# Fewer sums in the last pass of the first branch, its first tokens brought forward, and another order in the final block: one core of a hybrid GLA and Fourier layer

## What is computed

```python
h = _rmsnorm(x, norm_g) * (1 + scale) + shift
z = h @ w_in                      # q, k, v, gates, u, merge gates
...                               # gated linear attention: o; Fourier mixing: four
y_a = (o * silu(gate_a)) @ w_proj_a
y_b = (four * silu(gate_b)) @ w_proj_b
merged = sigmoid(mg_a) * y_a + sigmoid(mg_b) * y_b
x = x + gate * (merged @ w_out)
y = _rmsnorm(x, final_norm_g)
```

## Time and profile before

| what | value |
| --- | --- |
| median of three runs | 1940.96 us (1940.04 to 1943.69) |
| the profiled execution, its own time | 1941.48 us |
| its span, first to last instruction | 1939.7 us |
| busy: PE, DVE, ACT, POOL | 97%, 62%, 49%, 32% |
| mean granted clock of PE | 0.989 of full |

### The profile page before, as it was taken

The page is one execution under the profiler, slowest core; times in us unless marked ns, Lnnn a source line. Parts: engine busy times, 40 slices in busy tenths (PEclk is TensorE's granted clock), DMA queues, the critical chain, the costliest instruction groups (busy, mean ns, idle before and its releaser), DMA issues.

```text
span 1939.7 us, 30160 instructions
## 1 busy us (share of the span) xinstructions
PE 1876.0 (97%) x10393; PEld 1755.2 (90%) x10393; DVE 1211.3 (62%) x2103; ACT 941.2 (49%) x1961; POOL 620.3 (32%) x668
## 2 busy tenths in 40 slices
PE   7899999999999999999999998999999989998997
PEld 2899999999999999999999996888887889997886
DVE  4978887784444435644444455666665567599787
ACT  3565667653445446444455325777741242243343
POOL 0136644044334513345432000000931014233644
PEclk9999999999999999999999999999999999999998
DMA  7578878967788889778778969565447657765443
GB/s 286 209 271 291 284 284 317 369 245 255 249 280 284 254 302 349 240 227 290 261 263 291 351 194 362 211 236 218 167 184 238 217 169 228 254 206 176 163 163 130
DMA packets 170096, 483.24 MB, mean 249 GB/s; under 512 B 14880, under 2 KB 72666, under 8 KB 159964
## 3 DMA queue, kind: packets, MB, share of 16 engines
q1 hardware_dynamic: 156124, 430.99, 64.7%
q10 hardware_dynamic: 13824, 50.34, 6.5%
HBM read 316.64 MB, written 155.20 MB: 243 GB/s over the span
## 4 chain that ended last, share of the span: by engine, by line
PE 60%; DVE 8%; POOL 4%; DMA 3%; issue 3%; ACT 2%; SPq 0%; DVEq 0%; ACTq 0%; POOLq 0%
PE bank L2543 33%; PE bank L2889 7%; PE bank L2843 5%; PE bank L2707 3%; PE bank L2674 3%; PE bank L2772 2%; PE bank L2685 1%; PE bank L2696 1%; DMA x_st<-in_x 1%; POOL h_lo L1127 1%; DVE me_op L2164 1%; POOL yt L1261 1%; POOL yt L1258 1%; DVE me_s L2316 1%; DMA qd<-qk_dec 1%
## 5 line engine op out<-in xcount | busy, mean ns | idle before, releaser
L2543 PE MATMUL bank<-h_hi,w_op 128*128 128x384 f32 x4032 | 1053.3, 337 | 15.2 <-ACT outs L1340 4.6
L2543 PEld LDWEIGHTS bank<-h_hi,w_op 128*128 128x128 f32 x4032 | 732.6, 188 | 21.4 <-issue 21.3
L2543 PE MATMUL bank<-h_lo,w_op 128*128 128x384 f32 x2016 | 675.8, 335 | 0.0
L2543 PEld LDWEIGHTS bank<-h_lo,w_op 128*128 128x128 f32 x2016 | 380.3, 189 | 0.0
L1831 DVE TENSOR_TENSOR w_op<-w_raw,w_op 128x512 fp32r<-128x512 f32 x240 | 189.0, 788 | 96.8 <-ACT w_op L1300 93.4
L1152 POOL TENSOR_TENSOR decs<-decs,qk_s 128x192 f32<-128x192 f32 x192 | 123.3, 677 | 333.2 <-ACT decs L1374 332.9
L1300 ACT ACTIVATE w_op<-w_raw 128x512 fp32r<-128x512 f32 x240 | 149.3, 624 | 159.2 <-PE bank L2543 155.6
L2889 PE MATMUL bank<-op_a,a_op 128*128 128x384 f32 x1008 | 180.2, 340 | 9.1 <-issue 5.0
L2889 PEld LDWEIGHTS bank<-op_a,a_op 128*128 128x128 f32 x1008 | 179.3, 192 | 9.9 <-issue 5.4
L2922 PE MATMUL bank<-ow_op,me_op 128*128 128x512 f32 x756 | 176.8, 395 | 9.0 <-DVE u4o L2394 4.3
L2922 PEld LDWEIGHTS bank<-ow_op,me_op 128*128 128x128 f32 x756 | 142.8, 190 | 42.5 <-issue 7.7
(11 more groups left out here) (272 smaller groups left out, 2829.5 us busy)
## 6 DMA issues: line engine op xcount, KB each, us to landing
w_op<-wt_dram SPq DMA_DIRECT2D x192, 512.0 KB, 5.7
wt_dram<-w_op ACTq DMA_DIRECT2D x96, 512.0 KB, 4.6
w_raw<-in_w_in SPq DMA_DIRECT2D x48, 768.0 KB, 5.9
w_raw<-in_w_in SPq DMA_DIRECT2D x24, 1024.0 KB, 6.7
qk_dec<-decs SPq DMA_DIRECT2D x48, 384.0 KB, 6.5
mg_dram<-outs SPq DMA_DIRECT2D x24, 768.0 KB, 7.4
swap<-qk_s SPq DMA_DIRECT2D x48, 192.0 KB, 5.6
v_dram<-outs SPq DMA_DIRECT2D x24, 384.0 KB, 4.8
```

The lines of the kernel that those rows point to most:

```text
L2543: ins = pe.matmul(bnk, w_op[slot][:, part, k, :], h[:, j, k, :], start=(first and k == 0 and part == 0 and h is h_hi), stop=(k == HK - 1 a ...
```

## The change

**The output weights' sums** are no longer made from the whole weights in the last pass of the first branch. In windows 2, 6, 10 and 14 of the projection's second pass SP loads a quarter (one of the four k-tiles) of the four blocks of `w_out` (`load_ow_parts`), into places that the second pass leaves unused; in the window after, DVE makes the four sums of that quarter (`sum_ow_part`, 128x512 each), and in the one after that SP stores them to the new `ow_dram`. In the first branch's last pass SP then loads seven ready tiles (`load_ow`), three from `w_out` and four from `ow_dram`, where before it loaded four. The places of the tiles (`OW_LO`, `OW_HI`) are others, and high and low parts of the first two tiles are made a step earlier.

**The first branch's first tokens**: `top` is loaded at tile 26 of the second branch, not 29; the low parts of its last block are made at tile 24, not 27; `low_op(0)` and the first two `sum_tokens` stand behind tiles 34, 36 and 38, not behind tile 39.

**The final block**: DVE takes the quarter that frees the bank of PE's seventh product before the two sums that don't, and PE waits for one DVE instruction less.

```diff
+        ow_parts = Region(r1.at - 2048)("ow_parts", [P, 4, 512])
+        ow_first = Region(r1.at - 10240)("ow_first", [P, 512])
...
-        OW_LO = (A_LO[0], A_HI[2], A_LO[2], A_HI[0], A_HI[1], A_LO[1], A_LO[3])
-        OW_HI = (A_HI[3], A_LO[4], A_HI[4], A_LO[5], A_HI[5], A_LO[6], A_HI[6])
-        OW_STEP = (3, 4, 4, 5, 5, 6, 6)
-        ow_b11, ow_t2, ow_t1, ow_b12, ow_b21, ow_b22, ow_t4 = ow_src = [place(at, f"ow_src{j}", [P, HK, 512])
-                                                                      for j, at in enumerate(OW_LO)]
+        OW_LO = (A_LO[0], A_HI[0], A_LO[1], A_HI[1], A_LO[2], A_LO[3], A_LO[4])
+        OW_HI = (A_HI[2], A_HI[3], A_HI[4], A_LO[5], A_HI[5], A_LO[6], A_HI[6])
+        OW_READ = (0, 0, 1, 1, 2, 3, 4)
+        OW_STEP = (2, 3, 4, 5, 5, 6, 6)
+        ow_src = [place(at, f"ow_src{j}", [P, HK, 512]) for j, at in enumerate(OW_LO)]
...
+        OW_WINDOWS = (2, 6, 10, 14)
...
-        END = {"u2": AD + 1, "u4": AD + 2, "t12": AD + 4, "t21": AD + 6, "t22": AD + 8, "22": AD + 10, "11": AD + 12,
+        END = {"u2": AD + 1, "u4": AD + 2, "t22": AD + 4, "22": AD + 6, "t12": AD + 8, "t21": AD + 10, "11": AD + 12,
...
+            def load_ow_parts(part):
+                if part:
+                    sp.wait_ge(s_wr[1], 32 * part)
+                else:
+                    sp.wait_ge(s_wlo, split_count(NW - 1, NPROD - 1))
+                sp.dma_start(ow_parts[:, :, :], io["w_out"][:, :, part, :].rearrange("q p n -> p q n")).then_inc(s_wr[0], 16)
+
+            def store_ow_sums(part):
+                sp.wait_ge(s_owl, 4 * part + 4)
+                sp.dma_start(ow_dram[0, :, part, :], ow_first[:, :]).then_inc(s_wr[1], 16)
+                sp.dma_start(ow_dram[1:4, :, part, :].rearrange("q p n -> p q n"), ow_parts[:, 1:4, :]).then_inc(s_wr[1], 16)
...
+                    if p == 1 and w in OW_WINDOWS:
+                        load_ow_parts(OW_WINDOWS.index(w))
+                    elif p == 1 and w - 2 in OW_WINDOWS:
+                        store_ow_sums(OW_WINDOWS.index(w - 2))
...
-            def load_ow(k):
-                sp.dma_start((ow_b11, ow_b21, ow_b22, ow_b12)[k][:, :, :], io["w_out"][k]).then_inc(s_wr[k], 16)
+            def load_ow(j):
+
+                sp.wait_ge(s_y, product_a(NPROD * (NA - 1) + OW_READ[j], 3))
+                sp.wait_ge(s_wr[OW_SLOT[j]], ow_read(j) - 16)
+                src = (io["w_out"][0], ow_dram[2], ow_dram[0], ow_dram[3], io["w_out"][1], io["w_out"][2], ow_dram[1])[j]
+                sp.dma_start(ow_src[j][:, :, :], src).then_inc(s_wr[OW_SLOT[j]], 16)
...
-                if m == 29:
+                if m in (26, 29):
                     sp.wait_ge(s_bil, GROUPS * NB)
-                    load_tokens_a(0, 0)
-                    load_tokens_a(0, 1)
+                    load_tokens_a(0, int(m == 29))
...
-                        sp.wait_ge(s_y, product_a(NPROD * (NA - 1), 3))
                         load_ow(0)
-                        load_ow(3)
+                        load_ow(1)
+                    elif at == 4:
+                        load_ow(4)
+                        load_ow(5)
...
-                        sp.wait_ge(s_y, product_a(NPROD * (NA - 1) + 1, 3))
                         load_ow(2)
-                        load_ow(1)
+                        load_ow(3)
+                    elif at == 6:
+                        load_ow(6)
...
-                    for j in {4: (0,), 5: (1, 2), 6: (3, 4)}.get(i, ()):
+                    for j in {3: (0,), 4: (1,), 5: (2,), 6: (3, 4)}.get(i, ()):
...
+            def sum_ow_part(part, n):
+                b11, b21, b22, b12 = (ow_parts[:, q, :] for q in range(4))
+                out, x, y = ((ow_first[:, :], b12, b11), (b12, b12, b22), (b22, b22, ow_first[:, :]), (b21, b21, b22))[n]
+                if n:
+                    dve.wait_ge(s_owl, 4 * part + n)
+                else:
+                    dve.wait_ge(s_wr[0], 16 * (part + 1))
+                dve.tensor_tensor(out, x, y, ALU.subtract).then_inc(s_owl, 1)
...
+                        if p == 1 and w - 1 in OW_WINDOWS and 0 < j < 5:
+                            sum_ow_part(OW_WINDOWS.index(w - 1), j - 1)
...
-                if j == 3 and b + 1 < NB:
+                if (b, j) in ((0, 3), (1, 3), (2, 3), (3, 0)):
                     for g in range(GROUPS):
                         low_fourier(b + 1, g)
                 elif (b, j) in ((1, 1), (1, 6)):
                     for n in ((0, 1) if j == 1 else (2, 3)):
                         sum_a(n)
-                elif (b, j) in ((2, 2), (2, 6), (3, 1)):
-                    low_a(((2, 2), (2, 6), (3, 1)).index((b, j)))
-            low_op(0)
+                elif (b, j) in ((2, 2), (2, 6), (3, 3)):
+                    low_a(((2, 2), (2, 6), (3, 3)).index((b, j)))
+                elif b == NB - 1 and j == 2:
+                    low_op(0)
+                elif b == NB - 1 and j in (4, 6):
+                    sum_tokens(0, j // 2 - 2)
...
-                if i in (0, 2):
+                if step and i in (0, 2):
...
-                        sum_ow(0)
-                        sum_ow(1)
-                        sum_ow(2)
-                    elif i == 4:
-                        sum_ow(3)
+                        low_ow(0)
                         for n in range(3):
                             sum_me(0, n)
-                        low_ow(0)
-                    elif i == 5:
+                    elif i == 4:
                         low_me(0, 0)
                         low_ow(1)
+                    elif i == 5:
...
-            scaled_sum(y[0][:, sl[1]], u2o[:, :], 0, 1, END["u4"])
             dve.wait_ge(s_yst[1], 16 * (FINAL - 1))
+            scaled_sum(y[1][:, sl[1]], u4o[:, :], 1, 1, END["u4"])
+            end_quarter(1, 1, 3, 3, y[1][:, sl[1]], END["t22"])
+            scaled_sum(y[0][:, sl[1]], u2o[:, :], 0, 1, END["22"])
             scaled_sum(y[1][:, sl[0]], u2o[:, :], 1, 0, END["t12"])
-            scaled_sum(y[1][:, sl[1]], u4o[:, :], 1, 1, END["t21"])
-            end_quarter(1, 1, 3, 3, y[1][:, sl[1]], END["t22"])
             scale_rows(FINAL - 1, 1)
-            end_quarter(0, 0, 0, 4, x_end[0][:, sl[0]], END["22"])
+            end_quarter(0, 0, 0, 4, x_end[0][:, sl[0]], END["t21"])
...
-                    pe.wait_ge(s_owl, 4 + j + 1)
+                    pe.wait_ge(s_owl, 4 * 4 + j + 1)
...
-                    pe.wait_ge(s_ad, END["u4"] if j == 5 else END["22"])
+                    pe.wait_ge(s_ad, END["u4"] if j == 5 else END["22"] - 1)
```

35 lines of the change are left out of this document (11 added, 24 removed).

## The result

The changed kernel takes 1930.32 us (median of 4 runs, 1926.61 to 1931.80) beside 1941.43 for the kernel before (4 runs, 1940.04 to 1943.69): a ratio of 0.9939, with a 95% interval of 0.9922 to 0.9956. By the ratio that is 11.8 us faster, between 8.5 and 15.1 (the medians themselves differ by 11.1). In two later series of runs the same kernel stood at 0.9946 [0.9924, 0.9968] and 0.9945 [0.9932, 0.9958]. The forecast was 13.2 us and 1928; the range of 1922.5 to 1933 held the time. The profiled execution took 1931.80 us, its span 1930.0.

What follows compares the result with a forecast made beforehand. PE was busy 97% of the span, so time could be won only where it waits or runs slowly. 7.5 + 4.6 + 1.4 - 0.3 = 13.2 us off 1941.48 gave 1928.3, predicted as 1928 us; 8-in-10 range 1922.5 to 1933.

Steps and rivals of the forecast that it cites:

- Part A: Entry to the first branch: PE's 5.0 us wait and 2.5 us of slow clock behind it go; 7.5 us won.
- Part B: Last pass and first output block: `u4a` wait and its slow clock go, `u4o` wait grows; 4.6 us won.
- the long waits grow: First output block: PE's wait for `u4o` grows from 3.3 to 5.0 us.
- later small waits absorb: Output: PE's next two waits, 1.0 and 1.12 us, would absorb 2.1 us of the slow clock's cost.
- I count nothing; if they hold DVE, part B shrinks: Last pass: seven weight loads, 7 MB for 4, share the queue with DVE's gate tiles; no cost counted.
- a sign against itself: First output block: a `u4o` wait as before or gone, not about 5 us, would mean DVE's chain was misread.
- Rival 2: Heavier loads or the first output block give Part B back, PE's clock included: 1932 us; chance 15%.
- Part C: Final block: PE's 3.3 us wait goes and PE ends 6.0 us earlier, but the end comes only 1.4 earlier.
- Part D: Projection's second pass: 16 added sums, 13 us of DVE, and their transfers stay nearly hidden; 0.3 us lost.
- Rival 3: Entry to the first branch: gates, tokens and sums crowd, the second step waits: 1933 us, at worst 1935.5; chance 10%.
- rival 4: Projection: quarters of `w_out` arrive so late that DVE stands; slower, 1966 us; chance 4%.
- rival 1: DVE keeps nearly all it is given, so Part B gives 8 to 12 us: 1924 us, at best 1921; chance 10%.

Runs made afterwards that it cites:

- e8: The changed kernel with both loads of the first branch's first tokens at tile 29, as before the change; 0.9939 of the kernel before.
- a2_after: The changed kernel unaltered, run and profiled a second time; 0.9946 of the kernel before.
- a3_after: The changed kernel unaltered, run and profiled a third time; 1928.32 us, 0.9945 of the kernel before.
- e4: The changed kernel with the seventh weight tile's 1 MB load issued five merges later, behind the last gate tiles; 0.9940 of the kernel before.
- e3: The changed kernel with Part A and Part C taken back, so only the output weights' sums are changed; 0.9983 of the kernel before.
- e2: The kernel before with only the final block's order changed; 0.9997 of the kernel before.
- e10: The changed kernel with 32 sums in place of 16 in the projection's second pass, transfers unchanged; 1931.78 us, 0.9960 of the kernel before.
- e9: e6 with loads of weight tiles 2 and 3 moved behind the first block's merged tokens; 1924.06 us (0.9925 of the kernel before), again 1922.47 us (0.9914).
- e6: The changed kernel with e4's late load, and ACT making the first output weight's high part ahead of its copies; 0.9937 of the kernel before.

## Why the prediction was right, and where it was wrong

**Part A, 7.5.** Right, with its parts. PE's wait of 5.0 is gone in every profile with this part, and the clock is 1.00 at the start of the first branch. Alone it gave 6.8 [4.3, 9.3]. The condition named (three DVE instructions among the last tiles are covered by its wait for the gate) holds; e8 shows that they would be covered even with the old load.

**Part B, 4.6.** The step up to the output was right. The idle time behind ACT's high part was 4.39 (predicted 4.8), the `u4a` wait went (in the other two profiles 0.8 and 0.7 us of it are left), and the slow clock with it: the two slow stretches of the first branch and that wait should give 2.5 + 6.6 = 9.1 there, and the branch is 9.4 us shorter (7.5 in a2_after, 8.0 in a3_after). **The term that was mis-sized is what the output gives back.** The 13 products take 4.2 us more after than before, where the prediction had 1.7 + 0.3 = 2.0; it is 6.3 in a2_after and 5.3 in a3_after. For the first profile each of its three pieces can be read off:

| us | predicted | measured |
|---|---|---|
| the long waits grow | 3.3 to 5.0: 1.7 | 3.3 to 1.9 + 3.8: 2.4 |
| slow clock behind them | 2.5 | 3.2 |
| later small waits absorb | 2.1 | 1.0 + 1.1 to 0.7: 1.4 |
| given back | 2.0 | 4.2 |

The measured clock piece is what the waits leave of the 13 products: 45.7 - 6.4 - 35.9 = 3.4 after, 41.5 - 5.4 - 35.9 = 0.2 before. The windows with 0.84 and 0.85 above show where it is. The prediction gave part B a lower bound of 2 us for nearly this case (the clock costs 2.5, nothing absorbs it, "and the transfers delay DVE a little"), and counted 4.6 all the same. Two of the three profiles fall below that bound. The step that failed first is "I count nothing; if they hold DVE, part B shrinks", of the loads that share the queue with gate tiles. They held DVE for 3.5 us, and that made the new wait of PE (1.9 to 2.9) ahead of the `u4o` one; e4, without it, gives back 43.9 - 41.5 = 2.4, near the 2.0 predicted. The number argued from had been a mean rate over 35 us; what decides is one 1 MB load directly ahead of tiles with a lead of a few us.

The prediction named a sign against itself: a `u4o` wait "as before or gone". It is 3.8, 2.7 and 3.8 us beside 3.3 before and 5.0 foretold, so by its length alone the sign was nearly there. What grew is the sum of PE's waits up to and with `u4o`: 5.7, 5.6 and 6.0 us, and 4.9 in e4, where DVE has no gate tile to wait for. That DVE comes late there was foretold, and by about the right amount; that PE would stop at a second place ahead of it was not.

Part B is then 6.9 - 4.2 = 2.7 us in the first profile (9.4 less part A's clock of 2.5), -1.3 in a2_after and 0.2 in a3_after; the runs without parts A and C (e3) give 3.3 [1.2, 5.4]. Rival 2, that the first output block gives it all back, describes the two later profiles, and about half of the first.

**Part C, 1.4.** The mechanism was right, the size is at the upper end: 0.1 to 1.5 us by the profiles (e2 above), 0.6 [-1.2, 2.3] by time alone. What it wins beside the wait is the slow clock behind it, and the prediction took that from one trace. PE's 12 last matmuls run at full clock, and DVE's reads of PE's banks at the end do not wait for PE:

```profile
1922.51 1.06 ACT L1788 ACTIVATE junk<-yt 128x1024 bf16<-128x1024 f32 x1 [2.07 <-DVE yt L2472]
1922.59 0.69 DVE L2470 TENSOR_TENSOR p1o<-bank,res_gate 128x512 f32<-128x512 f32 x1
...
1924.22 0.63 ACT L1762 ACTIVATE junk<-yt 128x512 bf16<-128x512 f32 x1
```

The last squares of ACT wait for the row sum before them, as the prediction said.

**Part D, 0.3.** Not contradicted, not proved. The groups of DVE after:

```profile
L2041 DVE TENSOR_TENSOR ow_parts<-ow_parts 128x512 f32<-128x512 f32 x8 | 6.5, 809 | 0.0
L2041 DVE TENSOR_TENSOR ow_parts<-ow_parts,ow_first 128x512 f32<-128x512 f32 x4 | 3.0, 762 | 0.0
L2041 DVE TENSOR_TENSOR ow_first<-ow_parts 128x512 f32<-128x512 f32 x4 | 2.7, 686 | 5.4 <-DMA ow_parts<-in_w_out 5.4
```

12.2 us for 16 sums (13 predicted), with a mean of 0.76. The term that was mis-sized is the wait for the transfers. DVE stood 5.4 us in all, but 4.3 of it at one place, over the 3 that were allowed for each:

```profile
549.80 0.69 DVE L2041 TENSOR_TENSOR ow_first<-ow_parts 128x512 f32<-128x512 f32 x1 [4.32 <-DMA ow_parts<-in_w_out]
```

PE did not wait there (e10 above shows how near it was). Over the second pass its waits are 3.5 us, and 3.9 before. The prediction had also set the rule of the Trainium skill on the interface that POOL shares with VectorE (GPSIMD Engine Reference, "Specifications") against this part. The trace agrees as far as it goes: four of the 16 sums took 0.89 to 1.08 us, all four while POOL worked on `decs`; but others in the same stretches took 0.68 to 0.70, like the rest.

**Rival 3** (A does less) and **rival 4** (late quarters) didn't come: the four loads of the quarters landed 8.8 to 11.7 us after their issue, where PE would have been held from 13 on by the prediction's account. Of **rival 1** only e9 has something: to use DVE's idle time took three changes of order, and gave 6 us.

**Sum.** By the stages from the second branch on, the change won 11.8, 7.6 and 9.4 us in three profiles, by the ratios 11.8, 10.5 and 10.7. That is 1.4 to 2.7 us short of 13.2, and the errors of parts B and C both point that way: 1.9 us or more for B, up to 1.3 for C. The time fell inside the range because the range was wide enough for a part B of next to nothing, not because the sum had that part right.

## What to carry to other kernels

An engine's idle time that was seen to end with X can be only the first of several limits in a row: removing X moved 4 us of it to the next load (e6), and a gain clear of the scatter came only when that load was moved too (e9). When bulk loads share a queue with small tiles that pace an engine, cost each 1 MB load by what is issued within the next few us, not by mean rate. And where an early gain arrives at a stage which is short of another engine, predict what that stage gives back as a term of its own, its clock included. A slow stretch read from one trace is one draw: behind waits of 3.2 to 5.0 us it cost between nothing and 2.8 us in these kernels.

## What the runs showed that was not expected

- The time up to the second branch differed by 9.2 us between two executions of one kernel (1452.9 and 1462.1 us); in the changed kernel it was 1453.1 to 1458.4. That is as large as most effects here.
- The granted clock stayed at 1.00 behind a wait of 3.32 us in the kernel before, and behind 3.22 us in e2. Behind 3.77 us in the changed kernel it was below 1 in part of the next 10 us, and in e4 behind 3.85 us (first row below). But it also fell behind a wait of only 1.94 us in the changed kernel, and behind 2.95 us in e9 (second row). The length of the wait alone doesn't tell:

```profile
1750.00:1760.00 10.00, 10.00 (x39) 0.85 0.84 329
1746.00:1756.00 10.00, 9.02 (x33) 0.83 1.02 384
```

- The same 1 MB load of tokens took 9.7 us to land behind two others of 1 MB (e6) and 5.2 us without them (e9).
